# A decoder trunk kernel: eight heads' weights of the first tile in three rooms in turn and loaded ahead, some weights kept for later phases, the second tile's attention nine slots later

## The reference

```python
h = x
for layer in range(2):
    hn = rms_norm(h, norm_mix[layer])
    h = h + (hybrid_attention(hn, ...) if layer % 2 == 0 else conformer_conv(hn, ...))
    h = h + peer_ffn(rms_norm(h, norm_ffn[layer]), peer_w_q[layer], peer_subkeys[layer], peer_u[layer], peer_v[layer])
return rms_norm(h, norm_final)

# peer_ffn for 128 tokens (8 heads, 2 x 128 keys, 16384 experts, top 16):
q = (xc @ w_q).reshape(128, 8, 2, 128)
s = einsum('thcd,hcnd->thcn', q, subkeys)
s_top, i_top = top_k(s, 16)
cand = s_top[:, :, 0, :, None] + s_top[:, :, 1, None, :]
best, pos = top_k(cand.reshape(128, 8, 256), 16)
g, idx = softmax(best), the experts' numbers at pos
act = gelu(einsum('td,thkd->thk', xc, u_tab[idx]))
y = einsum('thk,thkd->td', g * act, v_tab[idx])
```

## Time and profile before

| | us |
|---|---|
| median of 3 runs | 1593.02 |
| lowest, highest | 1592.80, 1595.99 |
| the profiled execution | 1592.89 |
| its span in the trace | 1591.1 |

### The profile page before, as it was taken

How to read it: one execution, slowest core, us unless ns; L and a number is a source line. 1 busy time by engine, 2 the same in 40 slices (tenths; PEclk the granted TensorE clock), 3 DMA queues, 4 the chain that set the end, 5 groups by cost and what they waited for, 6 DMA issues and landing times.

```text
span 1591.1 us, 20460 instructions
## 1 busy us (share of the span) xinstructions
PE 1026.5 (65%) x6572; PEld 506.6 (32%) x6572; DVE 1100.9 (69%) x2959; ACT 597.0 (38%) x1794; POOL 599.9 (38%) x516
## 2 busy tenths in 40 slices
PE   7988676567657677666767677457577644444443
PEld 3545333223234345322234355223234401101000
DVE  3433757777455579999675479689876677767764
ACT  2323345453233334444343334334424523332321
POOL 0003234454313345555233444334444444434441
PEclk9999786776868788756688789656688855555555
DMA  9437889999999999999999999999999999999996
GB/s 397 148 101 304 316 339 419 419 419 419 408 417 415 416 419 394 410 394 407 419 413 415 415 419 417 419 418 404 395 408 401 405 420 419 420 419 419 421 419 266
DMA packets 94859, 617.00 MB, mean 388 GB/s; under 512 B 11040, under 2 KB 15136, under 8 KB 26144
## 3 DMA queue, kind: packets, MB, share of 16 engines
q0 software_dynamic: 73728, 536.90, 82.3%
q1 hardware_dynamic: 20304, 78.61, 12.6%
q10 hardware_dynamic: 720, 0.18, 0.0%
HBM read 614.61 MB, written 1.05 MB: 387 GB/s over the span
## 4 chain that ended last, share of the span: by engine, by line
DMA 37%; DVE 24%; PE 20%; issue 12%; ACT 5%; POOL 2%; SPq 0%; DVEq 0%; another core or an unknown queue 0%; POOLq 0%; ACTq 0%
DMA ring<-table_dram,idx 28%; DVE ring L1564 10%; PE bank L543 8%; DMA head<-heads_dram 6%; PE qpsum L543 5%; DVE arena L1449 5%; PE ypsum L543 4%; PE spsum L543 2%; ACT L980 2%; POOL ring L536 2%; DMA arena<-c_out_dram 1%; DMA arena<-heads_dram 1%; DVE topi L1498 1%; ACT ring L980 1%; ACT wts L980 1%
## 5 line engine op out<-in xcount | busy, mean ns | idle before, releaser
L536 POOL DMA_INDIRECT ring<-table_dram,idx x512 | 599.7, 1171 | 966.3 <-PE ypsum L543 699.0
L1564 DVE CUSTOM_DVE_ANT_0 ring<-xns,ring 128x1024 f32<-128x1024 f32 x512 | 623.0, 1222 | 316.3 <-DMA ring<-table_dram,idx 312.0
L543 PE MATMUL ypsum<-ring,wts 128*32 128x256 f32 x4096 | 426.4, 511 | 459.7 <-ACT wts L980 452.5
L980 ACT ACTIVATE gel<-dot 128x1 f32<-128x1 f32 x512 | 103.1, 201 | 756.1 <-DVE dot L1564 734.0
L543 PEld LDWEIGHTS ypsum<-ring,wts 128*32 128x32 f32 x4096 | 100.0, 126 | 708.4 <-ACT wts L980 644.5
L980 ACT ACTIVATE wts<-gident,gel 128x32 f32<-128x32 f32 x512 | 164.6, 321 | 16.9 <-ACT gel L980 0.2
L543 PE MATMUL qpsum<-head,hT 128*128 128x256 f32 (+1 forms) x368 | 115.1, 475 | 46.3 <-DMA head<-heads_dram 42.0
L980 ACT ACT_TABLE_LOAD x84 | 107.8, 1283 | 8.3 <-PE bank L548 6.8
L543 PEld LDWEIGHTS qpsum<-head,hT 128*128 128x128 f32 (+1 forms) x368 | 84.1, 237 | 75.4 <-issue 37.8
L1449 DVE SCALAR_TENSOR_TENSOR arena<-arena,cols 128x128 f32<-128x128 f32 x360 | 103.9, 344 | 0.7
L543 PE MATMUL bank<-hT,arena 128*128 128x128 f32 x512 | 75.2, 307 | 2.8 <-issue 2.8
(11 more groups left out here) (160 smaller groups left out, 1046.0 us busy)
## 6 DMA issues: line engine op xcount, KB each, us to landing
head<-heads_dram SPq DMA_DIRECT2D x42, 512.0 KB
ring<-w_in_dram SPq DMA_DIRECT2D x4, 2048.0 KB, 16.8
ring<-table_dram,idx POOLq DMA_INDIRECT x512
arena<-c_in_dram SPq DMA_DIRECT2D x4, 2048.0 KB, 23.1
arena<-heads_dram SPq DMA_DIRECT2D x7, 1152.0 KB
arena<-c_out_dram SPq DMA_DIRECT2D x6, 1024.0 KB, 9.6
arena<-w_out_dram SPq DMA_DIRECT2D x1, 4096.0 KB, 38.1
arena<-heads_dram SPq DMA_DIRECT2D x16, 256.0 KB, 4.1
```

The costliest lines, as they stand in the source:

```text
L536: pool.indirect_dma_start(out=row(b), out_offset=None, in_=table[:, :], in_offset=bass.IndirectOffsetOnAxis(ap=idx[R % 2][:, k:k + 1], axi ...
L543: return nc.tensor.matmul(o_, l, r, start=start, stop=stop, **kw)
L980: return nc.scalar.activation(out_, in_, func, **kw)
L1564: V.tensor_tensor_reduce(out=u, in0=xnr[G % 2], in1=u, scale=1.0, scalar=0.0, op0=ALU.mult, op1=ALU.add, accum_out=dot[:, k:k + 1]).then_i ...
```

## The change

Heads 0 to 7 all get weights outside the order of `load_head`: three rooms in turn, a (heads 0, 4, 7), b (1, 5) and the tile `head` (2, 6), and a fourth, d, for head 3 in parts of `kT`, `mkT` and `mqT` that tile 1's attention fills later. Their loads are issued in a new order. `HEAD_ORDER` changes in which order a phase takes its heads, so that the last head of phase 0 in `head` is the first of phase 1 (head 8), six blocks of head 7's weights are those of head 9 (`STAYED_K`), and the last head of phase 2 is the first of phase 3 (head 24). At the start of phase 1 the fourth piece of `cin` is loaded after head 9's product. The attention of tile 1 starts nine slots later in most of its steps; its pairs come every 6 slots in place of 7, and what ends it comes one slot later. VectorE gets a wait for head 5's scores at slot 14.

```diff
+HEAD_ORDER = [(4, 5, 6, 7, 0, 1, 2, 3), (2, 3, 0, 1, 4, 5, 6, 7), (0, 1, 2, 3, 4, 5, 6, 7), (7, 0, 1, 2, 3, 4, 5, 6)]
+STAYED, PART_STAYED, LAST_STAYED = HEADS, HEADS + 1, (PHASES - 1) * HEADS
...
 def head_no(H):
-    return (H % HEADS + QUAD * (H < HEADS)) % HEADS
+    return HEAD_ORDER[H // HEADS][H % HEADS]
...
+STAYED_K = 6
...
-PAIR_SLOT = [26 + 7 * q for q in range(PAIRS)]
+PAIR_SLOT = [34 + 6 * q for q in range(PAIRS)]
...
-NORM_SLOT = [93, 95, 95]
+NORM_SLOT = [94, 95, 95]
...
 def streamed(H):
 
-    return H >= QUAD and (H < (PHASES - 1) * HEADS or H % HEADS == 0)
+    return PART_STAYED < H < LAST_STAYED
...
-                   [part["qT"][:, 0:W2], part["qT"][:, W2:2 * W2], vmla[1][:, 0:W2], proj[1][:, CHUNK:2 * CHUNK]],
+                   [xnr[0][:, 0:W2], xnr[0][:, W2:2 * W2], vmla[1][:, 0:W2], proj[1][:, CHUNK:2 * CHUNK]],
...
-        first_q = [[left[:, 0:W2], left[:, W2:2 * W2], left[:, 2 * W2:3 * W2], o_[:, 0:W2]],
-                   [pp_[:, 0:W2], pp_[:, W2:2 * W2], part["qT"][:, 0:W2], part["qT"][:, W2:2 * W2]], early_q[0]]
-        first_q.append(first_q[0])
-        first_keys = [o_[:, W2:W2 + 2 * KEYS], o_[:, W2 + 2 * KEYS:W2 + 4 * KEYS], head[:, HEAD_K:HEAD_W], vmla[1][:, 0:2 * KEYS]]
+        room_a = [left[:, 0:W2], left[:, W2:2 * W2], left[:, 2 * W2:3 * W2], o_[:, 0:W2]]
+        room_b = [pp_[:, 0:W2], pp_[:, W2:2 * W2], part["qT"][:, 0:W2], part["qT"][:, W2:2 * W2]]
+        room_d = [kT[:, 0:4, P:SEQ], kT[:, 4:8, P:SEQ], mkT[:, :, P:SEQ], mqT]
+        keys_a, keys_b, keys_c = o_[:, W2:W2 + 2 * KEYS], o_[:, W2 + 2 * KEYS:W2 + 4 * KEYS], head[:, HEAD_K:HEAD_W]
+        first_q = [room_a, room_b, early_q[0], room_d, room_a, room_b, early_q[0], room_a]
+        first_keys = [keys_a, keys_b, keys_c, vmla[1][:, 0:2 * KEYS], keys_a, keys_b, keys_c, keys_a]
...
-        first_in = [sem(f"first_in{H}") for H in range(QUAD)]
+        first_in = [sem(f"first_in{H}") for H in range(HEADS)]
...
+            def load_piece(H, from_, to, signal):
+                at_ = head_no(H) * HEAD_W
+                sp.dma_start(head[:, from_:to], heads_in[H // (TILES * HEADS)][:, at_ + from_:at_ + to]).then_inc(signal, 16)
+            def load_head_a(H):
+                sp.wait_ge(head_taken, H - PART_STAYED)
+                load_piece(H, 0, HEAD_A, head_a_in)
+            def load_head_b(H):
+                full(sp, q_job(H - 1))
+                load_piece(H, STAYED_K * 2 * HALF if H == PART_STAYED else HEAD_A, HEAD_K, head_b_in)
+            def load_keys(H):
+                full(sp, s_job(H - 1))
+                load_piece(H, HEAD_K, HEAD_W, keys_in)
             def load_head(H):
-                layer, h, m = H // (TILES * HEADS), head_no(H), H - QUAD
-                before = H - 1 if m else H - 2
-                if m:
-                    sp.wait_ge(head_taken, m)
-                else:
-                    full(sp, q_job(before))
-                sp.dma_start(head[:, 0:HEAD_A], heads_in[layer][:, h * HEAD_W:h * HEAD_W + HEAD_A]).then_inc(head_a_in, 16)
-                full(sp, q_job(before))
-                sp.dma_start(head[:, HEAD_A:HEAD_K], heads_in[layer][:, h * HEAD_W + HEAD_A:h * HEAD_W + HEAD_K]).then_inc(head_b_in, 16)
-                full(sp, s_job(before))
-                sp.dma_start(head[:, HEAD_K:HEAD_W], heads_in[layer][:, h * HEAD_W + HEAD_K:(h + 1) * HEAD_W]).then_inc(keys_in, 16)
+                load_head_a(H)
+                load_head_b(H)
+                load_keys(H)
...
             for s in (2, 3):
                 for i in range(KD // 2):
                     load_early(s, i)
-            full(sp, PROJ_JOB[1][4])
-            load_gain(0)
-            full(sp, HEAD_AT[0] + 3 * (HEADS - 1))
-            for i in range(KD // 2):
-                load_early(1, i)
+            for i in range(3):
+                load_first(3, i)
             full(sp, MOBA_AT[0] + 1)
             for i in range(3):
                 load_first(0, i)
+            full(sp, PROJ_JOB[1][4])
+            load_gain(0)
+            for i in range(KD // 2):
+                load_early(1, i)
+            full(sp, HEAD_AT[0] + 3 * (HEADS - 1))
+            for i in range(2, 4):
+                load_first(1, i)
+            full(sp, HEAD_AT[0] + 3 * (ATTN_HEADS - 1))
+            load_first(3, 3)
             full(sp, HEAD_AT[0] + 3 * (ATTN_HEADS - 1) + 2)
             for i in range(2):
                 load_first(1, i)
             for H in range(2):
                 load_first_keys(H)
             full(sp, EARLY_Q)
-            for i in range(2, 4):
-                load_first(1, i)
             for i in range(4):
                 load_first(2, i)
             full(sp, EARLY_S)
             for H in (2, 3):
                 load_first_keys(H)
-            full(sp, q_job(0))
-            for i in range(4):
-                load_first(3, i)
-            for H in range(QUAD, HEADS + 1):
-                load_head(H)
+            for before, H in ((0, 4), (1, 5), (2, 6), (4, 7)):
+                full(sp, q_job(before))
+                for i in range(4):
+                    load_first(H, i)
+                full(sp, s_job(before))
+                load_first_keys(H)
             for p in range(PHASES):
                 if p == 2:
                     full(sp, CONV_AT[1] + J_GLU + KD - 1)
-                    for h in range(1, HEADS):
-                        sp.dma_start(kept[:, (h - 1) * HEAD_W:h * HEAD_W],
+                    for h in range(HEADS - 1):
+                        sp.dma_start(kept[:, h * HEAD_W:(h + 1) * HEAD_W],
                                      heads_in[1][:, h * HEAD_W:(h + 1) * HEAD_W]).then_inc(kept_in, 16)
                 full(sp, rep_jobs(p * GROUPS + 3)[1])
                 load_gain(p + 1)
                 if p == 0:
+                    n = KD * 2 * 256
                     sp.wait_ge(x_mixed, TILES)
-                    for j in range(4):
-                        n = KD * 2 * 256
+                    for j in range(3):
                         sp.dma_start(part["cin"][:, j * n:(j + 1) * n], c_in[:, j * n:(j + 1) * n]).then_inc(cin_in[j], 16)
                     load_conv_out(0)
+                    load_head_a(PART_STAYED + 1)
+                    load_head_b(PART_STAYED)
+                    load_keys(PART_STAYED)
+                    load_head_b(PART_STAYED + 1)
+                    sp.dma_start(part["cin"][:, 3 * n:4 * n], c_in[:, 3 * n:4 * n]).then_inc(cin_in[3], 16)
+                    load_keys(PART_STAYED + 1)
                 if p in (1, 2):
                     load_conv_bias(p - 1)
                     load_conv_out(p)
                 if p < 2:
-                    for H in range((p + 1) * HEADS + 1, (p + 2) * HEADS + 1):
+                    for H in range((p + 1) * HEADS + (3 if p == 0 else 1), min((p + 2) * HEADS + 1, LAST_STAYED)):
                         load_head(H)
...
-                if s == 8:
+                if s == 17:
                     latents(1)
-                if s in (11, 12):
-                    queries(1, s - 11)
-                if s in (15, 16):
-                    keys_values(1, s - 15)
-                if s == 18:
+                if s in (20, 21):
+                    queries(1, s - 20)
+                if s in (22, 23):
+                    keys_values(1, s - 22)
+                if s == 27:
                     turn_queries(1)
-                if s == 20:
+                if s == 29:
                     turn_keys(1)
-                if s == 22:
+                if s == 31:
                     turn_moba(1)
...
-                if H < QUAD:
+                if H < HEADS:
                     pe.wait_ge(first_in[H], 5 * 16)
                 elif streamed(H):
-                    pe.wait_ge(head_a_in, (H - QUAD + 1) * 16)
-                elif h == 1:
+                    pe.wait_ge(head_a_in, (H - PART_STAYED) * 16)
+                elif H == LAST_STAYED + 1:
                     pe.wait_ge(kept_in, (HEADS - 1) * 16)
                 for k in range(KD):
-                    if streamed(H) and k == KD // 2:
-                        pe.wait_ge(head_b_in, (H - QUAD + 1) * 16)
+                    if streamed(H) and k == KD // 2 or H == PART_STAYED and k == STAYED_K:
+                        pe.wait_ge(head_b_in, (H - STAYED) * 16)
                     at_ = (h - 1) * HEAD_W + k * 2 * HALF
-                    w = first_q[H][k // 2][:, k % 2 * 2 * HALF:(k % 2 + 1) * 2 * HALF] if H < QUAD else \
-                        wq_[:, k, :] if streamed(H) else kept[:, at_:at_ + 2 * HALF]
+                    if H < HEADS:
+                        w = first_w(H, k)
+                    elif H == PART_STAYED and k < STAYED_K:
+                        w = first_w(HEADS - 1, k)
+                    elif H > LAST_STAYED:
+                        w = kept[:, at_:at_ + 2 * HALF]
+                    else:
+                        w = wq_[:, k, :]
                     last = mm(bank[:, 0:2 * HALF], xnT[:, k, :], w, k == 0, k == KD - 1)
```

(49 more changed lines are left out.)

17 lines of the change are left out of this document (9 added, 8 removed).

## The result

| us | before | after |
|---|---|---|
| median | 1593.78 (4 runs, 1592.80 to 1595.99) | 1571.07 (4 runs, 1567.57 to 1571.79) |
| the profiled execution | 1592.89 | 1571.79 |
| its span | 1591.1 | 1570.0 |

After over before is 0.9853, with a 95% interval of 0.9841 to 0.9865: the kernel is 22.7 us faster.

A forecast was written before the change was run, and what follows sets the result against it. Bytes were taken to set the time from 240 us on, and loads standing in one order to cause gaps before. 1591.1 − 7.5 − 2.5 − 12.4 = 1568.7 us of span, so 1570.5 us; range 1563 to 1584.

The forecast's parts named there:

- (a): Heads 8 and 24 and six blocks of head 9 no longer loaded: 3.15 MB less in full stretches, 7.5 us.
- (b): Head 3's query weights, 1.05 MB, loaded before 100 us instead of among the gathers: 2.5 us.
- (c): 130 to 220 us: loads of heads 4 to 7 asked for earlier win 12.4 us of lost transfer time; bounds 0 and 20.4.
- the lost 20.4 us: Transfer time lost in 130 to 220 us: 29.11 MB took 90 us where 418 GB/s would need 69.6.
- (d): Second tile's attention nine slots later, pairs every six, VectorE's wait at slot 14: cost 0; up to 3 and 2 us.
- signs of a wrong forecast: Product 7 waiting over 4 us for weights, under 400 GB/s in 200 to 240 us, or the 300 us lead lost by the end.
- I leave 8 us of gaps: Gaps expected to remain from 130 us on: about 3 near 168 us, 1 or 2 at product 7, rest transfer edges.
- The first rival: Weights of heads 4 to 7 come too late or hold back gathered rows: 8 us wait, 1578.5 us; chance 0.17.
- The second: VectorE's three waits before 225 us only change place, so only the bytes are won: 1583 us; chance 0.12.
- The third: Product 6 stays late, so VectorE's new wait at slot 14 drains the ring: 1597 us; chance 0.05, with like ones.
- The fourth: The gaps in the early stretch vanish wholly, 3 us or less left: 1564 us; chance 0.08.

The follow-up runs named there:

- experiment 3: The changed kernel with heads 8 and 24 loaded again in full over themselves, 2.36 MB more: 1575.70 us, ratio 0.9889 to the kernel before.
- (5): The changed kernel with head 9's six kept blocks loaded again after product 8, 0.79 MB more: 1571.19 us, ratio 0.9850 to the kernel before.
- experiment 2: The changed kernel with head 3's four pieces of query weights asked for after product 0 again, ahead of head 4's: 1574.11 us, ratio 0.9884 to the kernel before.
- experiment 1: The changed kernel with weights of heads 4 to 7 asked for late, after products 2, 4, 5 and 6, same rooms: 1596.27 us, ratio 1.0026 to the kernel before.
- experiment 4: The kernel before with only tile 1's attention nine slots later and its pairs every 6 slots, loads as before: 1591.99 us, ratio 0.9992.
- experiment 10: The changed kernel run once more without edits, as the control beside later runs: 1568.89 us, ratio 0.9853 to the kernel before.
- Experiment 6: The changed kernel with products, turns and scores of heads 1 to 3 ahead of slot 0: 1569.08 us, ratio 0.9842 to the kernel before.

## Why the prediction was right

**The sum.** 22.4 us were forecast (1593.0 to 1570.5), 22.7 measured. Its terms, with what the runs gave each (by the medians, in brackets by the ratios; uncertain by 3 to 4 us):

| term | forecast | measured |
|---|---|---|
| (a) heads 8 and 24 | 5.6 | 4.6 (5.7) (experiment 3) |
| (a) head 9 | 1.9 | 0.1 (−0.5), so not told apart from nothing (5); 2.9 between two traces |
| (b) head 3 ahead | 2.5 | 3.0 (4.9), with a wait of its own in it (2) |
| (c) the lost 20.4 us | 12.4 | 16.0 in the trace (4.4 us of gaps are left); 25.2 (27.6) for the loads undone, with VectorE's new wait in it (1) |
| (d) attention, slot 14 | 0 | 0 (experiment 4; no idle at slot 14) |

That the sum hit 22.7 within 0.3 us is in part luck: (c) was too small by 3.6 us, and the two traces of the changed kernel end 21.1 and 26.1 us ahead of that of the kernel before. None of the signs of a wrong forecast came: product 7 waits for no weights, the rate in 200 to 240 us is 419 GB/s, and the lead is still there at the end.

**(a) held**, its bytes exactly: 613.86 MB, 613.9 forecast. The lead grows where it should: in the control's trace it goes from 21.6 us at slot 88 to 23.9 at slot 152 (head 9: 2.3) and from 23.6 at slot 248 to 26.5 at slot 280 (head 24: 2.9). In the first trace it grows by 0.8 and 3.1 there. Head 9's share alone is not shown by any time.

**(b) held** in its direction, with the caution of experiment 2 on its size. Rows of 512 bytes did no visible harm: product 3 starts at 151.09 and waits for nothing.

**(c) is right as a mechanism, and its size was somewhat too small.** Product 6 was forecast for about 180 and came at 179.23; VectorE's wait near 160 us stays, as forecast. What was mis-sized is the term "I leave 8 us of gaps": 4.4 were left. Product 7 ended at 190.3, not at 192 to 195, and the scores of head 7 came at 198.2, not 201. The dots of phase 0 were said to be some 17 us earlier at each slot; they are hardly earlier up to slot 16, and from slot 21 on by about 20 us. So at slot 40, where (b), (c) and head 8 are in (2.5 + 12.4 + 2.8 = 17.7 forecast), the lead is 19.6 us in the first trace and 21.3 in the control's. One part of it is in the earlier trace rows: product 6 took 6.82 us behind its wait, with a granted clock of 0.55 around it (183 to 198 us), mostly the level of 1.2 GHz, and takes 3.72 without the wait, at 1.00 in 179 to 183 us, the level of 2.4 GHz. In experiment 1 each of the three products behind a wait took 6.4 to 6.8 us again. In 181 to 188, 201 to 208 and 218 to 225 us there, where these products lie, the granted clock is 0.62, 0.58 and 0.58. That agrees with the rule of the Trainium skill, "TensorE: Matmul & The Clock Gate", Part 1, by which the clock falls when the engine idles; these 3 us stood beside the sum, not in it.

**The first rival** (weights too late or too early) did not come about: after shows no DMA wait at products 4 to 7. Experiment 1 puts its mechanism in by hand and has waits of 7.5 to 10.9 us each, near the 8 of its price, but three of them. The gathers were not held back either, though the taking of turns between queues ("DMA: Bandwidth & Descriptors", Queues, rings and completion order, in the Trainium skill) was its ground: whatever the weights of heads 4 and 5 take at 134 to 141 us, the rows have until VectorE's wait ends at 160.

**The second** (waits change place) fell: the 12.75 us are gone, and 8.89 became 1.90. **The third** (VectorE's wait at slot 14) did not come about, since product 6 was not late: no idle time there. But its mechanism is real. In experiment 1, where product 6 is late, the wait holds VectorE for 24.33 us, and the time is 1596.3 us, near the 1597 of this rival. **The fourth** (gaps vanish wholly) was nearest of the four: 4.4 us were left, 3 or less were its condition, and the time is 5 to 7 us above its 1564.

**Where the lead did not do as said.** 419 GB/s was forecast for 230 to 390 us; the first profile had 408 in 272 to 392 us, the control 416. Between slots 344 and 352 the first trace lost 2.3 us and the control 0.1. These are differences between executions of one program; the little that the block of output products adds in 360 to 400 us is told in experiment 10.

**Open.** What would win the last 4.4 us of 130 to 203 us. In after, 3.5 of them lie in 165 to 180 us, and the gathers at 165.77 and 172.40 wait 4.77 and 5.64 us for TensorE to free a place of `ring`: it adds slot 5 at 163.85, behind VectorE's wait, and then makes product 4. Experiment 6 moved this gap instead of closing it, for 0.7 us in all, (397 − 393) / 418 × 73; a run that shortens the wait and adds slot 0 on time is missing. That the control's trace ends 26.1 us ahead where the medians give 22.7 is also not settled; both profiles are single executions, and the earlier trace rows are of one as well.

## What to carry to other kernels

Where a kernel moves bytes at the link's rate nearly throughout, look for the stretch where it does not, and follow the wait there to the queue that issues the loads and to the room that they need. Here two things held head 6's load back. The smaller was the order: it was issued at 179.51 us behind a key load's wait, some 4 us after half of product 5 (173.66 to 177.35) had been made and the first half of the room was free. The larger was that the heads shared one room: with rooms in turn the same load goes out at 148.44. Rooms without the early request won nothing in experiment 1. Weights asked for some 30 us ahead, into places whose owner can come later, turned 20 us of lost transfer time into 4. Moving the owner later gained nothing by itself. 2.36 MB more in full stretches cost 4.6 to 5.7 us, about their transfer time of 5.6. And a wait that is free while its work comes in time (VectorE's at slot 14) can hold an engine for 24 us as soon as it does not.

## What the runs showed of the hardware

- The same program loses different stretches in different executions: 360 to 400 us at 391 GB/s in one and 412 in the other. The two traces of the changed kernel are 1.1 us apart at slot 24, 6.9 at slot 352 and 5.0 at the end. So a difference of a few us between two single profiles does not tell two kernels apart.
- A product of 16 matmuls behind a wait of 7.5 to 10.9 us for its weights took 6.4 to 6.8 us instead of 3.7, at five places in three kernels: the wait costs another 3 us after it has ended, and the granted clock around the products is 0.55 to 0.62. Product 4, without a DMA wait, took 6.12 us too, behind VectorE's long wait.
